# Expert results of a routed block: rows scattered to DRAM, or returned to token order by 0/1 products and added on chip

## The chip, the cores and the metric

One Trainium2 chip, one core. The metric is the device time of the whole program in microseconds (us). Times are the median of several executions; profiles are of one execution, on the same core.

## The reference

One transformer block with 512 tokens of width 1024, float32. The first half (a stick-breaking attention beside an RWKV-7 time mix, gates, an output product, a residual sum) gives `x1`. The change is in the second half, a mixture of experts:

```python
h = rmsnorm(x1, g2) * (1 + sc2) + sh2
# 4 groups of 8 experts: the group of the largest logit, in it the two best experts
combine = sum over the 2 choices of one_hot(expert) * (group_w * top_p)
y = 0
for e in range(32):
    hid = silu(h @ w_up1[e]) * (h @ w_up3[e])       # 1024 -> 512
    y = y + combine[:, e] * (hid @ w_down[e])       # 512 -> 1024
out = x1 + gt2 * rmsnorm(y, g3)
```

The weights of one expert are 1024x512, 1024x512 and 512x1024 float32, 6.29 MB; 32 experts, 201 MB in all, are read from DRAM once.

## The kernel before, in words

The program is five instruction streams (SP, Pool, ScalarE, VectorE, TensorE) that wait for each other on semaphores; their order is written out by hand.

**Blocks.** Each token has two choices, so there are 1024 rows to compute, put together in blocks of up to 64 rows (`CAP`) of one expert. Experts 0 to 29 have one block each (`LOOPED`), then come up to 18 overflow blocks (none with these inputs), then experts 30 and 31: 32 blocks. Three sets of buffers (`NSET`) are used in turn: block n uses set n mod 3. ScalarE stores the normalised rows of x1 to DRAM (`h2_rows`, L974). VectorE works out block and place of each choice from ranks, and TensorE sums two lists over the tokens (L2021): `idx_i`, the token of each place, and `dst_i`, the row of `choice_rows` to which the result goes.

**Loads.** SP loads each block's weights (`load_expert`, L439 to L456) in four parts of 1 MB (L444) and one of 2 MB (L448) or two of 1 MB (L452). The next load into a set is issued when TensorE has used the part: the first half of the up weights (`up_half`), the second (`up_done`), the down weights (`down_done`). All go through SP's one queue (q1).

**A block.** Pool gathers its rows by an indirect DMA (L627). TensorE turns them (`turn_rows`, L2031), VectorE scales them into `hgT` (L1470). TensorE makes the up products (L2042, 16 products of 128x512, each two entries in the trace), ScalarE takes silu (L988), VectorE multiplies (L1475), TensorE turns the product (L2049), VectorE copies it (L1477), and TensorE makes the down products (L2057). The two halves of the 1024 columns stand on partitions 0 to 63 and 64 to 127. ScalarE copies them to `yo` (L995), and Pool scatters `yo` to `choice_rows` in DRAM (L632), with a copy of the index ahead (L653, L663). The buffer of `yo` is used again when its last scatter has landed. TensorE's order is: up of block n, turning of n+1, transposes and down of n. Each set has PSUM banks of its own for up and down.

**The end.** The last block (31) is not scattered. SP waits for all scatters (L558) and reads `choice_rows` back, 4.2 MB (L562). ScalarE weighs the first choice (L1012), VectorE adds the weighed second (L1496), TensorE adds up that sum and the last block's rows in PSUM (L2085, L2091), ScalarE takes the squares' sum and its inverse root (L1016 to L1018), VectorE scales the row out of PSUM (L1501), and Pool (tiles 0 to 2, L673) or VectorE (tile 3, L1511) adds x1. Four stores (L565) end the program. x1 stays in SBUF throughout.

## Time and profile before

| | |
|---|---|
| three executions | 1134.23, 1134.31, 1136.68 us; median 1134.31 |
| the profiled execution | 1133.66 us |
| its span, first to last instruction | 1131.9 us |
| TensorE busy | 992.9 us (88%) |
| VectorE, ScalarE, Pool busy | 428.2, 287.3, 178.7 us |
| read from DRAM, written | 276.62 MB, 12.60 MB |
| queue q1 (SP) | 265.94 MB |
| queue q0 (Pool's indirect DMAs) | 8.40 MB, 5120 packets |

Window times count from the span's start. The expert loop begins at about 628 us; what stands ahead of it is not touched by the change but for buffers. A row of the chain view tells what the end of the program hung on at that moment: an engine's instruction (PE is TensorE), a DMA, or an issue on a queue (SPq is SP's). In group rows the columns are busy us and mean ns of one, then the idle us of the engine ahead of them with what ended it. In timeline rows the columns are start, length, engine, line, instruction, operands, count. DMA rates are in GB/s over all 16 DMA engines of the core; at more than 100% in a queue's share the packets' times overlap.

### The profile page before, as it was taken

The numbers are of one execution on the slowest core, as the hardware profiler recorded it, in microseconds if no ns is written. First come the engines' busy times: TensorE is split into PE (matmuls) and PEld (weight loads), VectorE is DVE, ScalarE is ACT, GpSimd is POOL, SyncE is SP. The second block draws the span as 40 slices with busy tenths as digits, with TensorE's granted clock in tenths as the row PEclk, the third lists the DMA queues.
The fourth block names the chain that finished last, engine by engine and source line by source line (L and its number), as shares of the span: only waits on it lengthen the run. The fifth ranks groups of instructions, "written<-read, shape, count | busy, mean of one in ns | idle before, by whom it ended". The sixth has DMA issues, their size and how long they took to land.

```text
span 1131.9 us, 17069 instructions
## 1 busy us (share of the span) xinstructions
PE 992.9 (88%) x7067; PEld 552.4 (49%) x7067; DVE 428.2 (38%) x853; ACT 287.3 (25%) x447; POOL 178.7 (16%) x239
## 2 busy tenths in 40 slices
PE   3999999999998999999997899977777788777876
PEld 2588478755556676546884433323322232222222
DVE  2477858444467341127437222222211221122124
ACT  3343462366641222245352000000000000000004
POOL 0100000322320100222601112211111111111002
PEclk9899999999999999999998899999999999999999
DMA  9676204205220002334329999999999999999996
GB/s 338 231 248 223 104 3 146 75 24 189 86 75 2 3 5 77 123 124 165 149 112 380 367 398 401 400 399 401 402 410 412 407 406 398 406 399 397 411 415 242
DMA packets 70803, 281.67 MB, mean 249 GB/s; under 512 B 9347, under 2 KB 18861, under 8 KB 46171
## 3 DMA queue, kind: packets, MB, share of 16 engines
q1 hardware_dynamic: 63408, 265.94, 60.6%
q0 software_dynamic: 5120, 8.40, 2.3%
q10 hardware_dynamic: 2218, 6.52, 1.6%
q8 instruction: 43, 0.70, 0.3%
q14 instruction: 14, 0.11, 0.0%
HBM read 276.62 MB, written 12.60 MB: 256 GB/s over the span
## 4 chain that ended last, share of the span: by engine, by line
PE 42%; SPq 30%; DVE 11%; DMA 8%; ACT 4%; issue 3%; POOL 1%; ACTq 0%; DVEq 0%; POOLq 0%
SPq L444 21%; PE ps L1718 7%; SPq L448 6%; PE ps L2042 4%; SPq L452 3%; PE ps L1729 3%; DMA ring<-in_w_up 2%; PE ps L2057 2%; PE ps L1587 2%; PE ps L1588 2%; PE ps L1589 2%; DMA arena<-in_w_mod 2%; PE ps L1830 2%; PE ps L1972 1%; DMA ring<-in_w_mod 1%
## 5 line engine op out<-in xcount | busy, mean ns | idle before, releaser
L2042 PE MATMUL ps<-arena 128*64 128x512 f32 x672 | 151.8, 596 | 35.1 <-DMA arena<-in_w_up 35.1
L1475 DVE TENSOR_TENSOR arena<-arena,ps 128x256 f32<-128x256 f32 x32 | 13.5, 421 | 370.6 <-ACT arena L988 370.6
L1718 PE MATMUL ps<-arena,ring 128*128 128x512 f32 x256 | 118.6, 604 | 0.0
L2042 PEld LDWEIGHTS ps<-arena 128*64 128x64 f32 x672 | 48.8, 137 | 136.6 <-issue 104.5
L2042 PE MATMUL ps<-ring,arena 128*64 128x512 f32 x352 | 79.9, 597 | 19.6 <-DMA ring<-in_w_up 19.6
L2057 PE MATMUL ps<-arena 128*64 128x512 f32 x336 | 78.4, 609 | 19.4 <-DMA arena<-in_w_down 14.2
L988 ACT ACTIVATE arena<-ps 128x256 f32<-128x256 f32 x32 | 12.3, 384 | 264.3 <-PE ps L2042 264.3
L1587 PE MATMUL ps<-h_upper,w_upper 128*128 128x512 f32 (+1 forms) x184 | 74.3, 404 | 4.4 <-POOL h_lower_first L573 4.1
L1589 PE MATMUL ps<-h_upper,w_lower 128*128 128x512 f32 (+1 forms) x184 | 72.7, 395 | 0.0
L1718 PEld LDWEIGHTS ps<-arena,ring 128*128 128x128 f32 x256 | 46.1, 190 | 48.8 <-issue 47.2
L1470 DVE TENSOR_SCALAR arena<-ps,par 128x64 f32<-128x64 f32 x256 | 67.2, 335 | 2.6 <-PE ps L2031 2.6
L995 ACT ACTIVATE arena<-ps 128x512 f32<-128x512 f32 x32 | 19.1, 597 | 182.5 <-PE ps L2057 182.5
L2042 PEld LDWEIGHTS ps<-ring,arena 128*64 128x64 f32 x352 | 25.8, 137 | 72.4 <-issue 38.7
L1588 PE MATMUL ps<-h_lower_first,w_upper 128*128 128x512 f32 (+1 forms) x138 | 55.0, 399 | 0.0
L2057 PEld LDWEIGHTS ps<-arena 128*64 128x64 f32 x336 | 25.2, 139 | 58.2 <-issue 38.8
L2057 PE MATMUL ps<-ring,arena 128*64 128x512 f32 x176 | 43.5, 640 | 10.7 <-DMA ring<-in_w_down 8.3
L653 POOL COPY dst_now<-dst_i 128x1 int32 x27 | 4.8, 178 | 297.2 <-ACT arena L995 297.2
L2031 PEld LDWEIGHTS ps<-cst,arena 64*128 64x128 f32 x256 | 30.7, 201 | 30.6 <-issue 30.6
L582 POOL TENSOR_SCALAR_AFFINE_SELECT arena<-arena 128x128 f32<-128x128 f32 x64 | 32.3, 539 | 66.2 <-DVE arena L1201 48.4
L1587 PEld LDWEIGHTS ps<-h_upper,w_upper 128*128 128x128 f32 (+1 forms) x184 | 34.7, 189 | 15.2 <-issue 6.3
L1589 PEld LDWEIGHTS ps<-h_upper,w_lower 128*128 128x128 f32 (+1 forms) x184 | 34.7, 188 | 8.3
L2031 PE MATMUL ps<-cst,arena 64*128 64x64 f32 x256 | 35.1, 278 | 3.9 <-DMA arena<-h_rows,idx_i 3.9
(388 smaller groups left out, 1605.8 us busy)
## 6 DMA issues: line engine op xcount, KB each, us to landing
arena<-in_w_up SPq DMA_DIRECT2D x84, 1024.0 KB, 28.8
ring<-in_w_up SPq DMA_DIRECT2D x44, 1024.0 KB, 29.1
ring<-in_w_down SPq DMA_DIRECT2D x11, 2048.0 KB, 35.0
arena<-in_w_down SPq DMA_DIRECT2D x11, 2048.0 KB, 32.4
arena<-in_w_down SPq DMA_DIRECT2D x20, 1024.0 KB, 28.4
ring<-in_w_mod SPq DMA_DIRECT2D x6, 2048.0 KB, 8.7
arena<-in_w_mod SPq DMA_DIRECT2D x6, 2048.0 KB, 9.4
ring<-in_w_in SPq DMA_DIRECT2D x6, 2048.0 KB, 8.4
```

The lines of the kernel that those rows point to most:

```text
L444: eng.dma_start(eset_up[u][i][:, 2048 * m:2048 * m + 2048], src).then_inc(w_in_sem[u][m], 16)
L448: eng.dma_start(dst, src).then_inc(w_in_sem[u][m], 16)
L452: eng.dma_start(eset_down[u][i], src[:, i, :]).then_inc(w_in_sem[u][m], 16)
L1470: last = TS(hgT[:, k, :], ps[:, 0, CAP * k:CAP * k + CAP], V("A1", k), V("SH1", k), ALU.mult, ALU.add)
L1587: mm(ps[0:m_, b, :], hi, h_hi[:, k, :], start=(k == 0), stop=False)
L1588: used = mm(ps[0:m_, b, :], hi, h_lo[k], start=False, stop=False)
L1589: last = mm(ps[0:m_, b, :], lo, h_hi[:, k, :], start=False, stop=(k == KD - 1))
L1718: last = mm(ps[:, bank, :], w[:, k, P * (n % 2):P * (n % 2) + P], hT[:, k, :], start=(k == 0), stop=(k == KD - 1))
L1729: last = mm(ps[:, 2 + n % 2, :], chunk("OSB", 4)[:, k, P * n:P * n + P], S4(s_q)[:, k, :], start=(k == 0), stop=(k == FT - 1))
L2031: last = tr(ps[:, 0, CAP * k:CAP * k + CAP], hv[:, k, :], ident[0:CAP, 0:CAP])
L2042: last = mm(ps[64 * hf:64 * hf + 64, UP_BANK[u], :].rearrange("p (m n) -> p m n", m=2), hgT[:, k, :], up_pair(u, k)[:, :, 256 * hf:256 * h ...
L2057: last = mm(ps[64 * hf:64 * hf + 64, DOWN_BANK[u], :], hv2[:, k % 2, k // 2, :], wd[:, k % 2, 512 * hf:512 * hf + 512], start=(k == 0), st ...
```

## The change

Results are no longer scattered to DRAM. For each block VectorE builds a 0/1 matrix `back` (slots of the block by 512 tokens) out of the tokens' slot numbers. The block's results, weighed by the router's factors, are multiplied by it on TensorE (one-pass float32r, four tiles of 128 tokens by 1024), and VectorE adds each tile to an accumulator in SBUF, `acc`. `acc` takes the place of x1, which is read back at the end from `h2_rows` and multiplied by its standard deviation. To keep more digits, the results stand as two parts, an upper (ScalarE) and a lower (VectorE), which both halves of the 128 partitions hold for the same 64 slots. The rows are gathered as before.

```diff
@@ SP: the end
-            sp.wait_ge(none_stored, 16)
-            for u in range(NSET):
-                sp.wait_ge(yo_stored[u], again * 16 + (32 if u == 0 else 16))
+            sp.wait_ge(up_done, NSET * again + NSET)
             for t in range(NT):
-                for ch in range(2):
-                    row = 2 * (T * ch + P * t)
-                    sp.dma_start(fin[t][:, ch, :], ye_dram[row:row + 2 * P, :].rearrange("(p h) n -> p (h n)", h=2)).then_inc(ring_in[t], 16)
+                sp.dma_start(x1_rows[t], h2_dram[P * t:P * t + P, :]).then_inc(h2_moved, 16)
@@ Pool
-            nc.gpsimd.indirect_dma_start(
-                out=ye_dram, out_offset=bass.IndirectOffsetOnAxis(ap=dst_i[:, MAXB - 1:MAXB], axis=0), in_=none, in_offset=None,
-                bounds_check=4 * T - 1, oob_is_err=False).then_inc(none_stored, 16)
+            pool.wait_ge(x1T_done, NT + 1)
+            nc.gpsimd.memset(S(3), 0.0)
+            nc.gpsimd.memset(S(4), 0.0).then_inc(zeroed, 1)
...
                     pool.wait_ge(yo_ready, NSET * it + (u + 1))
-                    nc.gpsimd.tensor_copy(dst_now[:, u:u + 1], dst_i[:, bass.ds(NSET * it + u, 1)]).then_inc(dst_link, 1)
-                    pool.wait_ge(dst_link, NSET * it + (u + 1))
-                    pool.sem_inc(register_pass, 1)
-                    scatter_rows(u, dst_now[:, u:u + 1])
+                    nc.gpsimd.tensor_copy(w_now[:, u:u + 1], w_slot[:, bass.ds(NSET * it + (NSET + u), 1)]).then_inc(w_now_ready, 1)
...
             for t in range(NT - 1):
                 pool.wait_ge(fin_row, t + 1)
-                nc.gpsimd.tensor_tensor(fin[t][:, 1, :], fin[t][:, 1, :], x1[:, t, :], ALU.add).then_inc(first_ready, 1)
+                pool.wait_ge(x1_back, t + 1)
+                nc.gpsimd.tensor_tensor(acc[:, t, :], acc[:, t, :], x1_rows[t], ALU.add).then_inc(first_ready, 1)
@@ ScalarE
-                A(yo[:, u, :], ps[:, DOWN_BANK[u], :], ACT.Copy).then_inc(yo_ready, 1)
+                for a, h in ((0, 0), (HD, 512)):
+                    last = A(yo[a:a + HD, h:h + 512], ps[a:a + HD, DOWN_BANK, :], ACT.Copy, scale=weight[a:a + HD, :])
+                last.then_inc(yo_upper, 1)
...
+            expert_act(NSET * again + (NSET + 1), w_slot[:, LAST:LAST + 1])
+            act.wait_ge(h2_moved, 2 * 16 * NT)
+            for t in range(2):
+                A(x1_rows[t], x1_rows[t], ACT.Copy, scale=std2[:, t:t + 1]).then_inc(x1_back, 1)
+            expert_act(NSET * again + (NSET + 2), w_slot[:, LAST + 1:LAST + 2])
             nc.scalar.preload_act_table_set("natural_log_exp_and_others")
...
             def square_sum(t):
-                link(A(fin_sq[:, t % 2, :].rearrange("p (h n) -> p h n", h=2), whole(t), ACT.Square, accum_out=V("ss", 12 + t)))
+                act.wait_ge(fin_ss, t + 1)
+                link(A(fin_sq, acc[:, t, :], ACT.Square, accum_out=V("ss", 12 + t)))
...
+            for t in range(2, NT):
+                A(x1_rows[t], x1_rows[t], ACT.Copy, scale=std2[:, t:t + 1]).then_inc(x1_back, 1)
@@ VectorE: ahead of the loop
-            TS(dst_i[:, :], where, 2.0, K("half"), ALU.mult, ALU.add).then_inc(dst_ready, 1)
+            link(STT(key, blk_, float(CAP), rr, ALU.mult, ALU.add))
+            for c in range(2):
+                TT(key_diag[:, c], ident3.broadcast_to((P, NT, P)), o1(key[:, NT * c:NT * c + NT]).broadcast_to((P, NT, P)),
+                   ALU.mult).then_inc(factor_ready, 1)
...
+            for i in range(N2):
+                TS(ohw[:, i, :], K("iota64")[:, 0:MAXB], blk_[:, i:i + 1], routf[:, i:i + 1], ALU.is_equal, ALU.mult).then_inc(factor_ready, 1)
@@ VectorE: in the loop
+            def add_back(t, sent):
+                dve.wait_ge(back_done, sent)
+                TT(two(acc[:, t, :]), two(acc[:, t, :]), ps[:, BACK_BANK[t]:BACK_BANK[t] + 2, :], ALU.add).then_inc(back_added, 1)
+            def yo_lower(blocks, weight):
+                dve.wait_ge(yo_upper, blocks)
+                for a, h in ((0, 0), (HD, 512)):
+                    o = HD - a
+                    last = STT(yo[o:o + HD, h:h + 512], ps[a:a + HD, DOWN_BANK, :], weight[a:a + HD, :],
+                               yo[a:a + HD, h:h + 512].bitcast(F32), ALU.mult, ALU.subtract)
+                last.then_inc(yo_ready, 1)
+            def back_rows(u, turn):
...
+                TS(b, key_rows[:, 0, :], slot, None, ALU.is_equal).then_inc(back_step, 1)
+                dve.wait_ge(back_step, turn_steps * turn + (2 * u + 2))
+                STT(b, key_rows[:, 1, :], slot, b.bitcast(F32), ALU.is_equal, ALU.add).then_inc(back_step, 1)
...
+            def expert_dve(before, rows, weight, first=False, last=False):
+                if not first:
+                    add_back(0, NT * before - 3)
+                    add_back(1, NT * before - 2)
+                rows()
+                dve.wait_ge(sil_ready, before + 1)
+                TT(hid, sil, ps[:, UP_BANK, 256:512], ALU.mult).then_inc(hid_ready, 1)
+                dve.wait_ge(ht_done, before + 1)
+                CP(hidT, ps[:, 1, 0:256]).then_inc(ht_ready, 1)
+                if not last:
+                    rows_turned_in(before + 2)
+                if not first:
+                    add_back(2, NT * before - 1)
+                    add_back(3, NT * before)
+                yo_lower(before + 1, weight)
@@ VectorE: the end (order: add 0, add 1, row 0, add 2, row 1, add 3, rows 2 and 3, sum of tile 3)
+            def last_added(t):
+                dve.wait_ge(fin_sum, t + 1)
+                TT(two(acc[:, t, :]), two(acc[:, t, :]), ps[:, FIN_BANK[t]:FIN_BANK[t] + 2, :], ALU.add).then_inc(fin_ss, 1)
             def scaled_row(t):
-                return STT(two(fin[t][:, 1, :]), whole(t), V("rs", 12 + t), row2, ALU.mult, ALU.mult)
+                return STT(two(acc[:, t, :]), two(acc[:, t, :]), V("rs", 12 + t), row2, ALU.mult, ALU.mult)
@@ TensorE
+            def send_back(u, t, bank):
+                for h in range(2):
+                    ins = mm(ps[:, bank + h, :], back[:, u, P * t:P * t + P], yo[:, 512 * h:512 * h + 512], start=True, stop=True)
+                return ins
             def expert_up: behind the first half of the up products
+                        if before is not None:
+                            pe.wait_ge(yo_ready, before)
+                            pe.wait_ge(back_added, NT * before - 3)
+                            for t in range(2):
+                                send_back((u - 1) % NSET, t, BACK_BANK[t]).then_inc(back_done, 1)
             def expert_down: behind the transposes
+                if before is not None:
+                    pe.wait_ge(back_added, NT * before - 1)
+                    for t in (2, 3):
+                        send_back((u - 1) % NSET, t, BACK_BANK[t]).then_inc(back_done, 1)
@@ the end
+            for t in range(NT):
+                send_back(1, t, FIN_BANK[t]).then_inc(fin_sum, 1)
```

The up products of all blocks now use one PSUM bank (2), the down products one (3). TensorE sums the slots' weights (16 products) ahead of turning the first rows, and spreads the tokens' slot numbers over the partitions (two products of 128x512) behind it.

## Rows read from the trace of the kernel before

**Rows 1.** page, busy share of the DMA engines in 40 slices

```profile
DMA  9676204205220002334329999999999999999996
```

**Rows 2.** the chain that ended last, in order of time: start us, us, what

```profile
641.33 6.87 PE ps L2042 x32
...
653.83 6.87 PE ps L2042 x32
...
703.95 2.00 SPq L452
```

**Rows 3.** timeline of SP's queue: start us, us, what, issues

```profile
766.68 6.92 SPq L448 DMA_DIRECT2D ring<-in_w_down  x1
...
910.70 6.56 SPq L448 DMA_DIRECT2D ring<-in_w_down  x1
```

**Rows 4.** timeline of Pool, its indirect transfers (L627 gather, L632 scatter)

```profile
1044.25 0.94 POOL L627 DMA_INDIRECT arena<-h_rows,idx_i  x1 [7.57 <-PE ps L2031]
...
1066.91 1.00 POOL L632 DMA_INDIRECT choice_rows<-arena,dst_now  x1 [0.88 <-POOL dst_now L663]
```

**Rows 5.** DMA view, 1020 to 1060 us, rate in 40 slices of 1 us

```profile
GB/s 418 418 434 426 381 258 270 389 393 418 410 451 426 410 401 418 467 401 442 397 410 291 287 410 410 410 467 410 373 254 320 451 426 418 401 418 434 418 434 410
```

**Rows 6.** DMA view, 1059:1066, then 1066:1074, queue 1: packets, MB, share

```profile
q1 hardware_dynamic: 408, 2.97, 101.7%
...
q1 hardware_dynamic: 443, 3.23, 96.7%
```

**Rows 7.** timeline, before and at the start of the expert loop

```profile
614.96 1.81 DVE L1431 TENSOR_SCALAR arena<-cst,rt 128x50 f32<-128x50 f32 x8
...
628.59 7.03 PE L2042 MATMUL ps<-ring,arena 128*64 128x512 f32 x31
```

**Rows 8.** groups by line and shape

```profile
L900 ACT ACTIVATE ring<-ps,par 128x512 f32<-128x512 f32 x8 | 5.5, 688 | 3.2 <-PE ps L1718 3.1
...
L1012 ACT ACTIVATE arena<-arena,routf 128x1024 f32<-128x1024 f32 x4 | 4.6, 1145 | 3.9 <-DMA arena<-choice_rows 3.9
...
L1294 DVE SCALAR_TENSOR_TENSOR arena<-ps,arena 128x512 f32<-128x512 f32 x4 | 2.8, 692 | 7.8 <-PE ps L1919 7.8
```

**Rows 9.** groups of Pool's instructions by line

```profile
L618 POOL MEMSET arena<- 128x2048 f32 x1 | 1.8, 1821 | 0.0
```

**Rows 10.** window 560:566, TensorE in the output products

```profile
560.00:566.00 6.00, 6.00 (x28) 1.00 0.00 0
```

**Rows 11.** timeline of expert 0

```profile
635.66 0.38 ACT L988 ACTIVATE arena<-ps 128x256 f32<-128x256 f32 x1 [6.27 <-PE ps L2042]
636.08 0.42 DVE L1475 TENSOR_TENSOR arena<-arena,ps 128x256 f32<-128x256 f32 x1 [7.95 <-ACT arena L988]
...
637.46 2.10 DVE L1470 TENSOR_SCALAR arena<-ps,par 128x64 f32<-128x64 f32 x8
...
637.68 3.65 PE L2057 MATMUL ps<-ring,arena 128*64 128x512 f32 x16 [0.59 <-DVE arena L1477]
```

**Rows 12.** timeline of the tail

```profile
1102.40 3.65 PE L2042 MATMUL ps<-arena 128*64 128x512 f32 x16 [1.90 <-DMA arena<-in_w_up]
...
1124.57 1.02 ACT L1016 ACTIVATE arena<-ps 128x1024 f32<-128x1024 f32 x1 [1.30 <-PE ps L2091]
...
1126.27 1.28 DVE L1501 SCALAR_TENSOR_TENSOR arena<-ps,par,raw 128x1024 f32<-128x1024 f32 x1 [1.69 <-ACT par L1018]
1127.59 1.23 DVE L1511 TENSOR_TENSOR arena<-arena 128x1024 f32<-128x1024 f32 x1
```

**Rows 13.** DMA view, 1100 to 1105 us, rate in 40 slices

```profile
GB/s 524 360 492 262 393 524 328 459 262 393 492 360 459 164 295 590 328 361 295 393 361 590 197 262 459 328 328 393 262 328 328 328 328 131 328 328 197 197 131 197
```

**Rows 14.** timeline, Pool and VectorE side by side in the mixer's end

```profile
528.44 1.29 POOL L611 TENSOR_TENSOR wo_lower<-arena,wo_upper 128x512 fp32r<-128x512 f32 x1 [1.81 <-ACT wo_upper L935]
...
528.90 1.38 DVE L1315 TENSOR_TENSOR ring<-ring,arena 128x512 f32<-128x512 f32 x1
```

**Rows 15.** one line of Pool, ns min/median/max

```profile
L673 POOL TENSOR_TENSOR arena<-arena x3: 2342/2346/3321, 1119.3 to 1124.8; 128x1024 f32<-128x1024 f32 x3
```

More of the change, by code:

```diff
@@ L136, in build @@
         wr = sb("wr", [P, KD, NG + E])
+        with (nc.sbuf_tensor("results", [P, D], F32R) as yo, nc.sbuf_tensor("key_rows", [P, 2, T], F32) as key_rows,
+              nc.sbuf_tensor("key_diagonals", [P, 2, NT, P], F32) as key_diag):
+            pass
         h_lo_first = sb("h_lower_first", [P, 6, T], F32R)
@@ L162, in build @@
             pass
+        with nc.sbuf_tensor("under_back", [P, 12 * 2048 + 512], F32), nc.sbuf_tensor("back", [P, NSET, T], F32R) as back:
+            pass
         arena = sb("arena", [P, 17, 2048])
@@ L1436, in _ @@
             link(TS(second, where, float(T), -float(T), ALU.is_ge, ALU.mult))
-            TT(idx_i[:, :], where[0:CAP], second[0:CAP], ALU.add).then_inc(idx_ready, 1)
+            TT(idx_i[:, :], where[0:CAP], second[0:CAP], ALU.add).then_inc(table_ready, 1)
             ov = ovb
@@ new lines, in _ @@
+            rows_turned_in(1)
+            dve.wait_ge(table_done, 3)
+            CP(key_rows[:, :, :], ps[:, BACK_BANK[1]:BACK_BANK[1] + 2, :]).then_inc(back_added, 1)
+            dve.wait_ge(table_done, 2)
+            CP(w_slot, ps[:, BACK_BANK[0], 0:MAXB]).then_inc(table_ready, 1)
+            dve.wait_ge(table_ready, 2)
+            dve.wait_ge(back_added, 1)
+            dve.wait_ge(zeroed, 2)
+            for u in range(NSET):
+                expert_dve(u, lambda: back_rows(u, 0), w_now[:, u:u + 1], first=(u == 0))
@@ new lines, in _, with back_rows_last @@
+            with dve.Fori(0, again) as it:
+                for u in range(NSET):
+                    expert_dve(NSET * it + (NSET + u), lambda: back_rows(u, it + 1), w_now[:, u:u + 1])
+            def back_rows_last(u):
+                b, slot = back[:, u, :], K("slot")[:, NSET + u:NSET + u + 1]
+                link(TS(b, key_rows[:, 0, :], slot, None, ALU.is_equal))
+                STT(b, key_rows[:, 1, :], slot, b.bitcast(F32), ALU.is_equal, ALU.add)
+            for u in range(E - LOOPED):
+                expert_dve(NSET * again + (NSET + u), lambda: back_rows_last(u), w_slot[:, LAST + u:LAST + u + 1],
+                           last=(u == E - LOOPED - 1))
@@ L2056, in expert_down @@
                     for hf in range(2):
-                        last = mm(ps[64 * hf:64 * hf + 64, DOWN_BANK[u], :], hv2[:, k % 2, k // 2, :],
+                        last = mm(ps[64 * hf:64 * hf + 64, DOWN_BANK, :], hv2[:, k % 2, k // 2, :],
                                   wd[:, k % 2, 512 * hf:512 * hf + 512], start=(k == 0), stop=(k == 3))
                 last.then_inc(down_done, 1)
+            for c in range(2):
+                ohr = rview(1168 + 256 * c, 256, 4)
+                for t in range(NT):
+                    pe.wait_ge(factor_ready, 2 * NT + 2 + NT * c + t + 1)
+                    for hf in range(2):
+                        last = mm(ps[64 * hf:64 * hf + 64, BACK_BANK[0], 0:MAXB], ohr[:, t, :], selw[:, c, t, :], start=(c == 0 and t == 0),
+                                  stop=(c == 1 and t == NT - 1))
@@ L2061, in _ @@
+            last.then_inc(table_done, 1)
             turn_rows(0, 1)
+            for c in range(2):
+                pe.wait_ge(factor_ready, 2 * NT + c + 1)
+                last = mm(ps[:, BACK_BANK[1] + c, :], K("ones"), key_diag[:, c].rearrange("p t q -> p (t q)"), start=True, stop=True)
+            last.then_inc(table_done, 1)
             pe.wait_ge(route_ready, 1)
-            steps = pe.value_load(nblk_i[0:1, 0:1], min_val=LOOPED // NSET, max_val=(LOOPED + MAXO) // NSET)
-            pe.wait_ge(sel_ready, 2 * NT + 1)
@@ L2065, in _ @@
-            for hf in range(2):
-                for t in range(NT):
-                    last = mm(ps[64 * hf:64 * hf + 64, 7, P * t:P * t + P], selw[:, t, :], ident, start=True, stop=True,
-                              skip_group_check=True)
-            last.then_inc(idx_done, 1)
-            with pe.Fori(0, steps) as it:
-                for u in range(NSET):
-                    expert_up(u, it)
-                    turn_rows((u + 1) % NSET, it + (1 if u + 1 < NSET else 2))
-                    expert_down(u, it)
@@ new lines, in expert @@
+            def expert(u, turn, before, last=False):
+                expert_up(u, turn, before)
+                if not last:
+                    turn_rows((u + 1) % NSET, turn + (1 if u + 1 < NSET else 2))
+                expert_down(u, turn, before)
+            for u in range(NSET):
+                expert(u, 0, u if u else None)
+            with pe.Fori(0, again) as it:
+                for u in range(NSET):
+                    expert(u, it + 1, NSET * it + (NSET + u))
+            expert(0, again + 1, NSET * again + NSET)
@@ L2107 @@
+            expert(1, again + 1, NSET * again + (NSET + 1), last=True)
+            pe.wait_ge(yo_ready, NSET * again + (NSET + 2))
+            pe.wait_ge(back_added, NT * NSET * again + (NT * (NSET + 1) + 1))
+            pe.sem_inc(register_pass, 1)
+            for t in range(NT):
+                send_back(1, t, FIN_BANK[t]).then_inc(fin_sum, 1)
 _INS = ['x', 'c', 'w_mod', 'b_mod', 'norm_gains', 'w_in', 'gate_bias', 'shift_mu', 'w0', 'w_decay_up', 'a0',
```

201 lines of the change are left out of this document (69 added, 132 removed).

## The prediction

> **What bounds the kernel now.** I read the page's slices first [rows 1]: the reader is to see that the DMA line stands at 9 through nearly all of the second half. Then the chain that ended last, in order of time [rows 2]: up to 704 us it runs through TensorE, one expert every 12.5 us (641.33 to 653.83), and from 703.95 on through SP's queue, which issues the loads of the expert weights. So two regimes: first TensorE eats what was loaded ahead, then it waits for weights. Third, SP's issues [rows 3]: the same load comes back after nine experts in 144.0 us, 16.0 us an expert. TensorE needs 12.5, so it has 3.5 us to spare. Fourth, what the DMA engines do with those 16 us [rows 4 to 6]. An expert's weights are 6.29 MB. In 1059 to 1066, with no indirect transfer, queue 1 moved 2.97 MB in 7 us (0.424 MB/us), which would be 14.9 us an expert [rows 6]. The missing 1.1 us are gather and scatter. The gather of 1044.25 had no scatter near it, and 4 to 6 us later the rate drops to 254 and 320 GB/s; the scatter of 1066.91 leaves no dip [rows 4, 5]. The scatter costs little more than its bytes.
>
> **Removed: the scatters.** Beside the scatter queue 1 moved 3.23 MB in 8 us where 3.39 were due [rows 6]: 0.38 us each. By bytes it is 32 rows of 4 KB, 0.13 MB, 0.31 us. I take 0.34. There are 31 ahead of the last weights (one an expert but the last): 31 x 0.34 = 10.5 us by which the last weights land earlier; ends 9.7 and 11.7. The end above, all of the 1.1 us (34), is spoken against by the gather's own dip; no gain at all would need DMA idle time, and the DMA line shows none [rows 1]. The Pool's issue and copies go too; nobody waits for them but the buffer of the same expert. The gather stays and keeps its dip.
>
> **Added before the loop.** VectorE makes eight more small products (the like took 1.81 us [rows 7]), a key and two 128x512 diagonals (0.69 each [rows 8]), and drops five instructions of about 1.7 us: it ends its routing some 2 us later. TensorE must form the weight table before it turns the first rows, so expert 0 starts at about 629.3 for 628.6 [rows 7]. The Pool clears x1's place (two 128x2048, 1.82 us each [rows 9], 3.6 together) where it issued a scatter before; VectorE waits for that only behind the first turned rows, some 6 us after the Pool may begin: hidden, and if it were not, the first experts would pay it out of the 3.5 us spare of each. The first buffers come free 0.7 us later; in the first 20 us the queue is only 1 to 2 us ahead, so DMA idles 0 to 1.5 us. I take 0.3.
>
> **Added in the loop.** Per expert TensorE gets eight one-pass products of 128x512; the output products show 28 in 6.00 us, 0.22 each [rows 10]. Four stand in the middle of the up products (0.9 us, plainly on TensorE's path), four behind the transposes. From the end of the product with silu (636.50) to the first down product (637.68) pass 1.2 us now [rows 11], half of them idle; the four lengthen that by about 0.4. Period: 12.5 + 0.9 + 0.1 + 0.4 = 13.9 us. VectorE gets four adds of 1024 (1.28 each [rows 12]), two compares of 512 and two subtractions (0.69 each [rows 8]), 7.9 us on top of the 0.42 for the product, as much for a copy, and 2.1 for the turned rows [rows 11]: 10.8 us. ScalarE copies twice with a weight (0.69 each [rows 8]) where it copied once. Who waits: the result is ready 1.4 + 1.4 + 0.2 = 3.0 us after the last down product, and TensorE asks for it after half of the up products, 3.4 us: hidden. Behind the first returns VectorE does 2.6 us of adds and 1.4 of compares, then must be free for the product with silu, which comes 4.8 us later (0.7 of returns, 3.6 of up products, 0.5 to the end of silu): hidden by some 0.8. Bounds: 13.4 if all of the second four hide, 16.0 if none of the eight overlap and each takes twice its 0.22. What decides: TensorE falls behind the weights at 15.0 us (637.3 + 31 P against silu of the last expert at 1102.1, below). At 13.9 it stays covered, with DMA as the cover.
>
> **Added in the tail.** I write the times as they would be without the DMA gain. The last weights end at 1105.0, where the rate has died away [rows 13]. x1 (2.1 MB) is issued behind them on the same queue, 5.0 us at queue 1's own rate [rows 6]: 1110.0. ScalarE waits for all four parts **before the last expert's silu**, then scales two of them (1.145 each [rows 8]): 1112.3. Before, that silu came at 1106.1 (1102.40 + 3.65 [rows 12]). So a wait of 6.2 us is new. Then: silu 0.38, product 0.42, 1.2 and 0.4 more to the first down product, down 3.65 [rows 11], two copies 1.4, two subtractions 1.4, first return 0.6: 1121.7. The table load and two scalings of ScalarE end beside that, at 1123.3. VectorE: two adds to 1124.3; square chain of tile 0 1.70 us (1124.57 to 1126.27 [rows 12]), 1125.0; scaled row 0 to 1126.3; add 2 to 1127.6.
>
> Here a port matters. The Pool's subtraction of 528.44 took 1.29 us; VectorE's sum of two SBUF operands that began at 528.90 was done only 0.55 us after the Pool's end, 1.38 us, where 512 elements with an operand in PSUM took 0.69 [rows 8, 14]. The scaled rows now read both operands from SBUF (before: PSUM), so they exclude the Pool's adds (2.34 us [rows 15]). Pool add 0: 1126.3 to 1128.7; row 1 to 1129.9; add 3 to 1131.2; Pool add 1 to 1132.3; row 2 to 1133.4, row 3 to 1134.7; Pool add 2, which waits by then, to 1137.1; VectorE's last add 1138.2; last output 3.1 us (span end less end of that add, 1128.82 [rows 12]): **1141.3**. With no exclusion it is 1137.5, so the port costs 3.8. The Trainium skill, SBUF — State Buffer, section "SBUF: two separate sides", says the same: VectorE and GpSimd share one port pair, the first to start keeps it for its whole instruction, and a VectorE instruction takes it if it has two SBUF inputs. By that rule the sum ends at 1141.3, by a port that is shared out evenly about 2 us sooner; the trace bears the rule out.
>
> **The sum.** 1141.3 + 0.3 - 10.5 = 1131.1 for a span of 1131.9: -0.8 us. The profiled execution took 1133.66, 0.65 less than the median of 1134.31, so I put it as 1134.31 - 0.8 = 1133.5. Gone are the last scatter's landing and the 4.2 MB of choice rows; what is late next is x1, and then the closing chain of VectorE and Pool.
>
> **Rivals.**
> Tail waits cheaper: x1 lands beside the last weights, or the port does not bite. For it: TensorE itself waits for the last weights. Against it: one queue, in order, and the row of the waiting sum [rows 14]. It would give 4 to 7 us: 1127 to 1130. Chance 0.25.
> Scatter dearer than its bytes: part of the dip is its doing where both stand together. Up to 34 us for 10.5; half of the way, -13: 1121. Against it: the gather alone has its dip, the scatter alone none [rows 4, 5]. Chance 0.08.
> Slower, the loop becomes TensorE's and VectorE's: products, subtraction and adds take turns, and the period passes 15.0 us. For it: five more handovers an expert, cover of only 0.4 to 0.8 us at two of them. At 15.5 us silu of the last expert comes at 637.3 + 31 x 15.5 = 1117.8, and 29.0 us later the end: 1146.8, +14.9: 1149. Chance 0.12.
> The DMA time of the scatters does not come back (idle gaps by late buffers eat it): 1141.6, +9.7: 1144. Chance 0.13.
> My forecast 0.42.
>
> **How the numbers follow.** About 0.3%, 3.4 us, is what a measurement here can tell from no change; 0.8 us is within it. Faster 0.25 + 0.08 = 0.33, same 0.42, slower 0.12 + 0.13 = 0.25. The range leaves out most of the dearest scatter and most of the slow loop: 1124 to 1145. The forecast's own range is 1131 to 1137.
>
> **What would show it.** Right: the DMA line full up to the last weights, SP's same load coming back in 15.6 to 15.7 us, up products of TensorE waiting for weights from about expert 15 on, the last weights some 10 us earlier, ScalarE idle 6 us before the last silu, scaled rows of over 2 us beside the Pool. Wrong: chain through TensorE and VectorE to the end (loop bound), DMA below 9 in the expert stage, no wait for x1, or a period under 15.4 us (scatter dearer).

## The result, and the profile after

| | before | changed |
|---|---|---|
| median | 1134.81 us | 1138.90 us |
| lowest to highest, of 7 each | 1134.23 to 1136.68 | 1138.63 to 1140.87 |
| the profiled execution | 1133.66 | 1140.87 |
| its span | 1131.9 | 1139.3 |

The ratio is 1.0038, interval 1.0026 to 1.0049: slower by some 4 us. 1133.5 was forecast, no change; the result lies within the range, but the time moved, and upwards. In the profiled execution the sum said 1131.1 for the span and 1139.3 was measured: 8.2 us are to be found. Part of that is spread between executions: the profiled one of the changed kernel is the longest of its seven, 2.0 us over the median, and the one before lies 1.2 us under its own. A second profile of the changed kernel, taken with the experiments, has a span of 1137.6 us, and the 1.7 us between the two lie ahead of the first gather.

The page of the changed kernel, its engines, its DMA line, queue 0 and the costliest new group:

```profile
PE 1045.1 (92%) x7311; PEld 584.2 (51%) x7311; DVE 666.9 (59%) x1126; ACT 311.3 (27%) x478; POOL 147.6 (13%) x206
...
DMA  9676203215220002433439999999999999999971
...
q0 software_dynamic: 2560, 4.20, 1.4%
...
L1455 DVE TENSOR_TENSOR arena<-arena,ps 128x1024 f32<-128x1024 f32 x124 | 145.4, 1213 | 53.3 <-PE ps L2068 53.3
```

The second half of the DMA line is as full as before [rows 1], but the last two slices are 7 and 1 where they were 9 and 6: the tail is longer and has nothing to move. Half of queue 0's bytes are gone. VectorE is 239 us busier and TensorE 52 us, and neither is the price: the chain that ended last, in order of time, shows why.

```profile
759.04 3.43 PE ps L2084 x16
...
773.21 3.43 PE ps L2084 x16
...
815.78 4.87 SPq L452
...
1078.07 6.29 SPq L562
1084.41 21.42 DMA arena<-h_rows
...
1106.91 1.13 ACT arena L984
```

One expert on TensorE, from up product to up product, is 14.17 us (759.04 to 773.21; 13.9 forecast, 12.5 before [rows 2]). At 815.78 the chain passes to SP's queue, as it did at 703.95 before. So the loop is still the weights' and not VectorE's. At the other end stands what is new: the chain no longer comes out of the last scatter and the reading of `choice_rows`, it comes out of x1 (`h_rows`, SP's L562) through ScalarE's scaling (L984). The timeline of the tail:

```profile
1095.89 3.65 PE L2084 MATMUL ps<-arena 128*64 128x512 f32 x16
...
1105.85 2.19 ACT L984 ACTIVATE arena<-arena,ST 128x1024 f32<-128x1024 f32 x2 [13.81 <-DMA arena<-h_rows]
...
1108.07 0.38 ACT L967 ACTIVATE arena<-ps 128x256 f32<-128x256 f32 x1
...
1108.96 0.70 PE L2091 MATMUL ps<-cst,arena 128*128 128x128 f32 x2 [9.41 <-DVE arena L1487]
...
1111.30 4.76 PE L2103 MATMUL ps<-arena 128*64 128x512 f32 x16
...
1120.02 2.35 DVE L1526 TENSOR_TENSOR arena<-arena,ps 128x1024 f32<-128x1024 f32 x2 [0.98 <-PE ps L2068]
...
1125.35 2.47 DVE L1531 SCALAR_TENSOR_TENSOR arena<-arena,par,raw 128x1024 f32<-128x1024 f32 x1
...
1131.41 3.31 POOL L654 TENSOR_TENSOR arena<-arena 128x1024 f32<-128x1024 f32 x1 [1.16 <-DVE arena L1531]
...
1132.56 3.25 DVE L1542 TENSOR_TENSOR arena<-arena 128x1024 f32<-128x1024 f32 x1
```

The last up products end at 1099.54 (1095.89 + 3.65), 6.5 us earlier than before (1106.05 [rows 12]). Silu, which needs nothing else, comes at 1108.07: 8.5 us behind them, because ScalarE waits for x1 first. TensorE is idle for 9.41 us, and the last down products behind that take 4.76 us for 3.65 before. Then the scaled row of 2.47 us and the last sum of 3.25 us are the instructions that the Pool's adds hold off, as forecast.

The granted clock of the same stretches (columns: window, its length, busy us of the engines, granted clock, DMA share, GB/s):

```profile
1099.00:1108.00 9.00, 0.55 (x4) 0.00 (x0) 0.00 (x0) 2.15 (x2) 0.00 (x0) 0.74 0.52 209
1108.00:1112.00 4.00, 3.04 (x8) 1.80 (x10) 2.29 (x4) 0.42 (x2) 0.00 (x0) 0.50 0.00 0
```

In TensorE's idle time the granted clock falls (0.74 is the mean of that window) to 0.50, the lower level (1.2 GHz), and the turning and the first down products are made there.

The timeline of the start, between the first gather and expert 0:

```profile
619.62 1.12 POOL L624 DMA_INDIRECT arena<-h_rows,idx_i  x1 [58.23 <-DVE idx_i L1409]
...
623.20 1.83 POOL L633 MEMSET arena<- 128x2048 f32 x1
...
623.82 3.94 DVE L1437 TENSOR_SCALAR SAs<-cst,rt,routf 128x50 f32<-128x50 f32 x8
...
626.88 1.95 PE L2112 MATMUL ps<-SAs,arena 128*64 128x50 f32 x32 [5.24 <-DVE SAs L1437]
...
629.83 3.18 PE L2118 MATMUL ps<-key_diagonals,cst 128*128 128x512 f32 x4
```

Expert 0 starts at 632.95, not at 629.3. The eight factor products took 3.94 us where the like took 1.81 before [rows 7], just while the Pool cleared x1's place; TensorE waited 5.24 us for them, and its key products took 3.18 us. The buffers of the first experts come free later, and the DMA view of 626 to 646 us (40 slices of half a us) shows the gap that this leaves:

```profile
DMA  2109259899899899998900098889999999999999
GB/s 90 41 25 213 33 164 377 377 442 442 361 492 459 360 475 410 410 475 344 426 33 0 0 148 197 254 344 393 459 410 426 410 410 492 393 410 475 393 426 393
```

From 636.5 to 637.5 us nothing moves, and little on either side. In 628 to 650 queue 1 carried 7.69 MB, for 8.67 before.

### The profile page after: what moved, and what is told of

It is laid out like the page before. It is cut to its first block, busy times and chain, and to the rows that moved or that the text cites. A ratio compares the mean times of both kernels' runs of the same rounds, so it can differ in the third digit from the quotient of the medians.

```text
span 1139.3 us, 17967 instructions
## 1 busy us (share of the span) xinstructions
PE 1045.1 (92%) x7311; PEld 584.2 (51%) x7311; DVE 666.9 (59%) x1126; ACT 311.3 (27%) x478; POOL 147.6 (13%) x206
## 4 chain that ended last, share of the span: by engine, by line
PE 51%; SPq 23%; DVE 12%; DMA 6%; ACT 4%; issue 3%; POOL 1%; DVEq 0%; ACTq 0%
SPq L448 15%; PE ps L2084 8%; PE ps L1749 7%; SPq L452 5%; PE ps L2103 5%; PE ps L1760 2%; PE ps L2068 2%; SPq L456 2%; DMA arena<-h_rows 2%; PE ps L1618 2%; PE ps L1619 2%; PE ps L1620 2%; DMA arena<-in_w_mod 2%; PE ps L1861 2%; PE ps L2062 1%
## 5 line engine op out<-in xcount | busy, mean ns | idle before, releaser
L1455 DVE TENSOR_TENSOR arena<-arena,ps 128x1024 f32<-128x1024 f32 x124 | 145.4, 1213 | 53.3 <-PE ps L2068 53.3
L2084 PEld LDWEIGHTS ps<-arena 128*64 128x64 f32 x672 | 47.4, 137 | 104.2 <-issue 99.2
L970 ACT ACTIVATE results<-ps,ST 64x512 fp32r<-64x512 f32 x64 | 43.6, 682 | 181.9 <-PE ps L2103 181.5
L2084 PE MATMUL ps<-ring,arena 128*64 128x512 f32 x352 | 79.9, 596 | 4.7 <-DMA ring<-in_w_up 4.7
L2068 PE MATMUL ps<-results,back 128*128 128x512 f32 x256 | 77.5, 425 | 3.2 <-DVE results L1462 3.2
L1462 DVE SCALAR_TENSOR_TENSOR results<-ps,ST,results 64x512 fp32r<-64x512 f32 x64 | 48.0, 750 | 46.5 <-ACT results L970 46.0
L2068 PEld LDWEIGHTS ps<-results,back 128*128 128x128 f32 x256 | 44.4, 193 | 35.2 <-issue 27.6
L645 POOL COPY ST<-ST 128x1 f32 x27 | 4.9, 183 | 336.2 <-DVE results L1462 336.2
L2103 PEld LDWEIGHTS ps<-arena 128*64 128x64 f32 x336 | 23.1, 138 | 45.4 <-issue 36.9
L1618 PEld LDWEIGHTS ps<-h_upper,w_upper 128*128 128x128 f32 (+1 forms) x184 | 34.5, 188 | 15.3 <-issue 6.3
```

The costliest lines, as they stand in the source:

```text
L1455: TT(two(acc[:, t, :]), two(acc[:, t, :]), ps[:, BACK_BANK[t]:BACK_BANK[t] + 2, :], ALU.add).then_inc(back_added, 1)
L1462: last = STT(yo[o:o + HD, h:h + 512], ps[a:a + HD, DOWN_BANK, :], weight[a:a + HD, :], yo[a:a + HD, h:h + 512].bitcast(F32), ALU.mult, ALU ...
L1618: mm(ps[0:m_, b, :], hi, h_hi[:, k, :], start=(k == 0), stop=False)
L2068: ins = mm(ps[:, bank + h, :], back[:, u, P * t:P * t + P], yo[:, 512 * h:512 * h + 512], start=True, stop=True)
L2084: last = mm(ps[64 * hf:64 * hf + 64, UP_BANK, :].rearrange("p (m n) -> p m n", m=2), hgT[:, k, :], up_pair(u, k)[:, :, 256 * hf:256 * hf + ...
L2103: last = mm(ps[64 * hf:64 * hf + 64, DOWN_BANK, :], hv2[:, k % 2, k // 2, :], wd[:, k % 2, 512 * hf:512 * hf + 512], start=(k == 0), stop= ...
```

## The experiments

They ran in three sets, each with its own executions of the kernel before; a ratio is to those. In the expectations, theory A is the account drawn from these two traces, that the named cause costs what is written there; B is that it costs nothing and the time goes elsewhere. The table puts what their traces say side by side, all counted from the first gather's issue, so that the stage ahead, which ends between 616.4 and 621.1 us in these executions, drops out (each number is a difference of two timeline rows, the last one of the span's end and silu). (Expert 0 of the kernel before begins with an entry of its own at 628.27 us, ahead of the 31 of [rows 7].) Each row of times is one profile, and the table shows how far profiles differ where no edit bears on the number: with the start untouched, the last up products end between 479.92 and 482.08 us, and with the tail untouched the stretch from silu to the end takes 30.58 to 31.34.

| kernel | ratio to before (interval) | start of expert 0 | end of last up products | last silu | from silu to the end |
|---|---|---|---|---|---|
| before | 1 | 9.28 | 487.06 | 487.11 | 25.80 |
| changed | 1.0038 (1.0026 to 1.0049) | 13.33 | 479.92 | 488.45 | 31.23 |
| changed, again | 1.0052 (1.0039 to 1.0066) | 13.36 | 479.92 | 488.43 | 31.26 |
| x1 later | 0.9953 (0.9935 to 0.9970) | 13.92 | 480.78 | 480.83 | 29.15 |
| rows in PSUM | 1.0010 (0.9998 to 1.0022) | 13.92 | 482.08 | 490.60 | 28.39 |
| warm tail | 1.0035 (1.0022 to 1.0048) | 13.50 | 480.96 | 489.47 | 29.58 |
| Pool clears later | 1.0042 (1.0027 to 1.0058) | 11.32 | 479.98 | 488.50 | 31.34 |
| warm start | 1.0052 (1.0033 to 1.0070) | 13.00 | 480.69 | 489.20 | 30.85 |
| both start edits | 1.0037 (1.0024 to 1.0050) | 10.31 | 478.14 | 486.64 | 30.58 |
| x1 later, rows in PSUM | 0.9917 (0.9904 to 0.9930) | 13.31 | 481.32 | 481.37 | 26.23 |
| all four | 0.9898 (0.9879 to 0.9918) | 10.42 | 479.17 | 479.22 | 25.71 |
| before, no scatters | 0.9897 (0.9880 to 0.9913) | 9.86 | 478.73 | 478.78 | 25.63 |

**ScalarE's wait for x1, moved behind the last expert's copies.**

```diff
@@ ScalarE
             expert_act(NSET * again + (NSET + 1), w_slot[:, LAST:LAST + 1])
-            act.wait_ge(h2_moved, 2 * 16 * NT)
-            for t in range(2):
-                A(x1_rows[t], x1_rows[t], ACT.Copy, scale=std2[:, t:t + 1]).then_inc(x1_back, 1)
             expert_act(NSET * again + (NSET + 2), w_slot[:, LAST + 1:LAST + 2])
             nc.scalar.preload_act_table_set("natural_log_exp_and_others")
...
+            act.wait_ge(h2_moved, 2 * 16 * NT)
+            x1_scaled(0); x1_scaled(1); square_sum(0); square_sum(1); x1_scaled(2); square_sum(2); square_sum(3); x1_scaled(3)
```

> The changed kernel, with ScalarE's wait for x1 and all four scalings of x1 moved behind the last expert's copies. Theory A (the wait for x1 holds up the last expert): silu of the last expert comes at about 1099.7 instead of 1108.1 us, TensorE no longer idles 9.4 us and its last down products take 3.65 instead of 4.76 us, so the end comes 9 to 11 us earlier: 1128 to 1130 us. Theory B (the end hangs on x1's transfer itself, whoever waits for it): the wait comes back at the sums with x1, the gain is under 4 us: 1135 or more. Theory C (the longer expert loop is the cause of the loss): the last expert's up products are late already, gain under 2 us: 1137 or more.

Median 1129.88 us. The timeline of its tail:

```profile
1093.55 3.65 PE L2090 MATMUL ps<-arena 128*64 128x512 f32 x16
...
1097.25 0.38 ACT L967 ACTIVATE arena<-ps 128x256 f32<-128x256 f32 x1 [7.56 <-PE ps L2090]
...
1099.50 3.65 PE L2109 MATMUL ps<-arena 128*64 128x512 f32 x16
...
1104.60 1.28 ACT L983 ACT_TABLE_LOAD   x1
1105.90 2.19 ACT L994 ACTIVATE arena<-arena,ST 128x1024 f32<-128x1024 f32 x2
```

Silu comes 0.05 us behind the up products. The down products take 3.65 us, since TensorE no longer stands idle ahead of them. And when ScalarE gets to x1, it starts right behind the table load: x1's landing is hidden altogether. By the ratios the wait cost 9.6 us (0.0085 x 1135); the table has 7.6 us of that at silu (488.45 to 480.83) and 2.1 behind it. The changed kernel's second ratio, 1.0052 from another set, would make it 11.2. That one wait is more than twice the whole loss.

**The last rows kept in PSUM.** The last add, the scaled row and, for tile 3, its sum with x1 take one operand from PSUM, as the kernel before did.

```diff
@@ VectorE
-                TT(two(acc[:, t, :]), two(acc[:, t, :]), ps[:, FIN_BANK[t]:FIN_BANK[t] + 2, :], ALU.add).then_inc(fin_ss, 1)
+                TT(whole(t), two(acc[:, t, :]), whole(t), ALU.add).then_inc(fin_ss, 1)
...
-                return STT(two(acc[:, t, :]), two(acc[:, t, :]), V("rs", 12 + t), row2, ALU.mult, ALU.mult)
+                return STT(whole(t) if t == NT - 1 else two(acc[:, t, :]), whole(t), V("rs", 12 + t), row2, ALU.mult, ALU.mult)
```

> The changed kernel, with the last sums kept in PSUM, so that the square and the scaled rows read PSUM and one SBUF operand; same instructions, same counts. Theory A (VectorE and Pool exclude each other where VectorE has two SBUF operands): scaled rows 1 and 3 take 1.28 us again (2.47 for row 1 now), the last sum 1.2 instead of 3.25, the end 3.5 us earlier: 1135.4. Theory B (the rows are long because of something else, or are not on the path): the lengths stay and the end moves by under 1 us: 1138 or more.

Median 1136.84 us. The timeline of its tail:

```profile
1124.69 6.98 POOL L657 TENSOR_TENSOR arena<-arena 128x1024 f32<-128x1024 f32 x3 [84.26 <-DVE arena L1534]
1125.64 1.28 DVE L1534 SCALAR_TENSOR_TENSOR arena<-ps,par,raw 128x1024 f32<-128x1024 f32 x1
...
1131.13 1.22 DVE L1545 TENSOR_TENSOR arena<-ps,arena 128x1024 f32<-128x1024 f32 x1
```

The same scaled row takes 1.28 us beside the Pool for 2.47, the last sum 1.22 for 3.25, and the Pool makes its three adds in one go. 3.2 us by the ratios (0.0028 x 1135), 2.8 by the table: the port was forecast at 3.8. The table's figure is too low, for the last down products of this profile took 5.35 us for 4.76. From the first of the last adds on (1120.34 us, 1120.02 in the changed kernel) the end comes 3.4 us sooner.

**TensorE kept busy while ScalarE waits for x1.**

```diff
@@ TensorE: the last expert
-            expert(1, again + 1, NSET * again + (NSET + 1), last=True)
+            expert_up(1, again + 1, NSET * again + (NSET + 1))
+            for _ in range(9):
+                mm(ps[:, 0, :], K("ones"), cst[:, 0:512], start=True, stop=True, skip_group_check=True)
+            expert_down(1, again + 1, NSET * again + (NSET + 1))
```

> The changed kernel, with nine unused products of 128x512 between the last expert's up products and its transposes, where TensorE idles 9.4 us (wait for x1). Nothing else is moved. Theory A (the granted clock falls in that idle time and lengthens what follows): last down products 3.65 instead of 4.76 us, the returns behind them shorter, the end 1.5 to 2 us earlier: 1137. Theory B (the products are long because of something else): no change, 1139. The difference between this run and the one with x1's wait moved tells how much of that wait's price is the clock.

Median 1139.34 us. Its clock by windows, the columns as above:

```profile
1099.00:1108.00 9.00, 9.00 (x24) 3.48 (x20) 0.47 (x1) 1.49 (x2) 0.00 (x0) 1.00 0.59 240
1108.00:1112.00 4.00, 2.53 (x13) 1.37 (x14) 2.23 (x4) 1.08 (x2) 0.00 (x0) 1.00 0.00 0
```

The clock stays at 1.00 (2.4 GHz) where it was 0.50, and the stretch from silu to the end is 1.65 us shorter in the trace (29.58 for 31.23). The last down products take 3.65 us for 4.76. That is the price of the clock, and it stands in no term of the forecast; against all profiles with an untouched tail (30.58 to 31.34) it is 1.0 to 1.8 us. In the medians it can't be told from nothing (1.0035 for 1.0038): the forecast gain of 1.5 to 2 us is shown in the trace alone.

**The Pool clears x1's place only when VectorE's factors are ready.**

```diff
@@ Pool
             pool.wait_ge(x1T_done, NT + 1)
+            pool.wait_ge(factor_ready, 4 * NT + 2)
             nc.gpsimd.memset(S(3), 0.0)
```

> The changed kernel, with Pool's two memsets of the accumulator held back until VectorE has made the eight weight factors; one wait more, nothing else. Theory A (a memset of Pool shuts VectorE out of the port while it runs): the eight small products take 1.8 us instead of 3.94, the first expert begins about 2 us earlier (631 instead of 633), DMA idles less at 636 to 639, and the end comes 1.5 to 2 us earlier: 1137. Theory B (the gap in the DMA rate comes from the gathers or from the order of loads, not from the late start): the small products get shorter, but the end does not move by over 0.7 us.

```profile
622.66 1.79 DVE L1438 TENSOR_SCALAR SAs<-cst,rt,routf 128x50 f32<-128x50 f32 x8
...
624.58 1.80 POOL L634 MEMSET arena<- 128x2048 f32 x1 [2.52 <-DVE SAs L1438]
...
626.07 3.78 PE L2119 MATMUL ps<-key_diagonals,cst 128*128 128x512 f32 x4
...
629.78 7.91 PE L2085 MATMUL ps<-ring,arena 128*64 128x512 f32 x32
```

In this timeline of its start the eight products take 1.79 us: the memsets beside them were what held them. (That they do it through a port is the expectation's account; the run shows the hold and not the way.) Expert 0 starts 2.0 us earlier. But TensorE still works at the lower clock (keys 3.78, expert 0's up products 7.91 for 7.09), and neither the end of the last up products (479.98) nor the median (1140.21 us) moves. The mechanism is shown, and the gain in time that A expected is missed.

**Four more unused products ahead of the weight table.**

```diff
@@ TensorE
-            idle_products(2)
+            idle_products(6)
```

> The changed kernel, with four more unused products of 128x512 on TensorE ahead of the weight table, where it idles 5.2 us. Theory A (the clock falls in that idle time): the key products take 1.9 us instead of 3.18, they end before the first rows are scaled, the first expert begins 0.8 us earlier, the end 0.5 to 0.8 us earlier: 1138.2. Theory B (they wait for something else): no change, or later if the unused products hold up the table.

Median 1141.71 us: no gain. VectorE's factors still take 3.95 us, and TensorE has run out of its unused products before they come. The key products take 3.54 us (3.18 in the changed kernel), with the granted clock at 0.56 in 630 to 633 us: the edit did not keep the clock up where they stand, so by itself it says nothing of what the clock costs there.

**Both start edits together, and the changed kernel once more.**

> The changed kernel with the two edits ahead of the loop together (Pool's clearing held back, four more unused products ahead of the weight table); each alone moved nothing. Theory A (each alone is covered by the other: late factors or slow key products): the first expert begins 10.5 us after the first gather's issue instead of 13.3, DMA moves about 1 MB more from 628 to 650 us, and the end comes 2 to 2.5 us earlier than the changed kernel of this call. Theory B (what DMA idles at the start it does not lose in the end): start earlier, end within 0.7 us.

> The changed kernel as it is, for comparison on the same chip. 1138.9 us, ratio to the kernel before 1.0038, if nothing depends on the chip.

The timeline of the start and the DMA view of 626 to 646 us, with both edits:

```profile
621.68 1.79 DVE L1438 TENSOR_SCALAR SAs<-cst,rt,routf 128x50 f32<-128x50 f32 x8
...
625.52 1.98 PE L2119 MATMUL ps<-key_diagonals,cst 128*128 128x512 f32 x4
...
627.79 7.09 PE L2085 MATMUL ps<-ring,arena 128*64 128x512 f32 x32 [0.29 <-DVE arena L1447]
```

```profile
DMA  5799999999998999999899999999999999999999
GB/s 115 279 393 442 393 475 393 426 426 442 426 442 377 475 401 369 254 246 295 328 426 426 442 393 426 426 410 442 426 410 377 426 410 442 410 442 393 426 426 442
```

Factors 1.79, keys 1.98, expert 0 at 10.31 us from the gather for 13.36. The gap is gone, only the gather's own dip is left, and queue 1 carried 8.68 MB in 628 to 650 for 8.00 in the changed kernel of the same set. The last up products end 1.8 us earlier (478.14 for 479.92). The ratios are 1.0037 and 1.0052, 1.7 us apart, but their intervals overlap: the 1.8 us is the traces', one of each.

**The two tail edits together.**

> The changed kernel with the two edits of the tail together (x1's wait behind the last copies, last sums in PSUM). Theory A (the two prices add): 9.6 + 3.2 = 12.8 us less than the changed kernel of this call, about 1126. Theory B (one hides the other): under 11 us less.

Median 1125.89 us; against the changed kernel in the same set 15.3 us (0.0135 x 1135), against its first ratio 13.7. The single edits add to 12.8, so they don't overlap. From silu to the end 26.23 us are left, 0.43 more than before the change.

**The kernel before without its scatters.** 31 of 32 scatters are taken out (the one left is the first, of zeros), and with them ScalarE's wait for their landing; SP then waits for the results of expert 30 and reads `h2_rows` twice where it read `choice_rows`. The results of 31 experts are left out of the output.

```diff
@@ Pool
-                nc.gpsimd.indirect_dma_start(
-                    out=ye_dram, out_offset=bass.IndirectOffsetOnAxis(ap=index, axis=0), in_=yo[:, u, :], in_offset=None,
-                    bounds_check=4 * T - 1, oob_is_err=False).then_inc(yo_stored[u], 16)
+                pass
@@ SP
-                    sp.dma_start(fin[t][:, ch, :], ye_dram[row:row + 2 * P, :].rearrange("(p h) n -> p (h n)", h=2)).then_inc(ring_in[t], 16)
+                    sp.dma_start(fin[t][:, ch, :], h2_dram[P * t:P * t + P, :]).then_inc(ring_in[t], 16)
```

> The kernel before without its 32 scatters of results (the first one, of zeros, stays) and without the waits for their landing; in their place at the end SP waits for the result of the last but one expert and reads h2_rows twice, the same 4.2 MB; the results of 31 experts are left out. It prices the scatters by themselves. Theory A (a scatter costs the DMA engines its bytes, 0.34 us each): the last up weights land 9 to 11 us earlier than at 1102.4, and the end 10 to 11 us plus what the last scatter's landing cost (about 7 us, of which the reads take part): 1117 to 1124 us. Theory B (the scatter's DMA time was idle time anyway, or is returned only in part): the last up weights land under 6 us earlier. Theory D (the scatter is also the cause of part of the dips at the gathers): over 13 us earlier.

Median 1123.76 us. One line each of the DMA view of 650 to 1050 us, of the kernel before, of this one and of the changed one (columns: packets, MB, share of 16 engines):

```profile
q1 hardware_dynamic: 20892, 153.98, 96.3%
```

```profile
q1 hardware_dynamic: 21339, 157.36, 98.4%
```

```profile
q1 hardware_dynamic: 21337, 157.40, 98.4%
```

26 scatters lie in that stretch. Without them queue 1 carries 3.38 MB more, or 3.42 in the changed kernel; the scatters' own bytes are 26 x 0.131 = 3.4 MB. So a scatter costs its bytes and no more, 0.31 us at 0.42 MB/us, and the changed kernel gets all of that back in the loop. The profiles of the changed kernel and its variants carry 156.73 to 157.57 MB in this stretch, which makes it 0.25 to 0.33 us. The last up products start at 1092.87 us for 1102.40, 9.5 us earlier, of which 1.2 are the stage ahead: 8.3 by the table. The expectation also counted on the last scatter's landing, and got nothing there: from silu to the end it is 25.63 us for 25.80.

**All four edits.**

> Four edits to the changed kernel together: x1's wait and scalings behind the last expert's copies; the last sums kept in PSUM; Pool's clearing of the accumulator held back until VectorE has made the weight factors; four more unused products of TensorE ahead of the weight table. Theory A (what the scatters gave back was lost in these four places, and the expert loop itself costs nothing): 1138.9 less 10 less 3.5 less 2.3 to 3: 1122 to 1124 us, some 11 us under the kernel before. Theory C (the expert loop of the change costs time itself): no lower than 1130.

Median 1124.18 us, ratio 0.9898 (0.9879 to 0.9918): 11.6 us faster than the kernel before, and the version that beats both. From silu to the end it needs 25.71 us, as little as the kernel before, and silu stands 7.9 us earlier.

## Why the prediction was wrong

It was wrong by its sign; its mechanism held, and four sizes didn't. In the profiled executions, point by point:

- **Removed: the scatters.** Right in kind: their bytes took time of the DMA engines that the weights need, and the changed kernel's loop gets it back. Mis-sized: 0.34 us each was taken between 0.31 and 0.38, and 31 counted. Measured 0.31, the lower end, and the last of the 31 (issued at 1097.48 us) moves its bytes from 1100 us on, beside the very last weights only. From 650 to 1095 us queue 1 gains 3.90 MB on the kernel before, 9.3 us for 10.5. **1.2 us.**
- **Added before the loop.** This step failed by its reasoning. The memsets were called hidden, because nobody waits for them; what they do to VectorE beside them was not asked. The prediction had VectorE and the Pool in each other's way in the tail, but only for instructions with two SBUF operands, and these products have one. Nor is the stage ahead of the loop untouched but for buffers, as the description of the kernel before has it: the memsets, the factor products and the key products stand in it. The memsets held the factor products (3.94 us for 1.79), TensorE stood idle for 5.24 us and went on at the lower clock, expert 0 started at 632.95 for 629.3, and the DMA engines idled. 0.3 us was taken. Counted 31 us on from the first gather, queue 1 has moved 82.10 MB for 83.33 before: 1.23 MB, 2.9 us at 0.42 MB/us, **2.6 us** more. With both start edits it has moved 83.00 MB, for 82.17 in the changed kernel of the same set: 2.0 us of it come back there. Another **0.6 us** is the first gather itself, 619.62 for 618.99, where executions of one kernel differ by more (617.91 in the second profile of the changed kernel).
- **Added in the loop.** Right. 14.17 us a period against 13.9, TensorE covered by the weights from 816 us on, about expert 13 (15 forecast). The groups by line of 650 to 1050 us show the cover shrink as it should, here the largest one, after first and before second: TensorE's idle time ahead of these up products fell from 28.0 to 9.8 us. With the other groups of up and down products, the idle time ended by a weight's DMA is 14.3 us for 67.7.

```profile
L2084 PE MATMUL ps<-arena 128*64 128x512 f32 x576 | 131.0, 596 | 9.8 <-DMA arena<-in_w_up 9.1
```

```profile
L2042 PE MATMUL ps<-arena 128*64 128x512 f32 x544 | 122.8, 596 | 28.0 <-DMA arena<-in_w_up 28.0
```

- **Added in the tail, x1's landing.** The wait was found and put in the right place, and is the largest single cost, 9.6 us with all that hangs on it. It was sized as 5.0 us of bytes behind the last weights. At 1095 us queue 1 still had 3.56 MB to move, 2.10 of them x1: at full rate that ends at 1103.5. ScalarE's go came at 1105.85. The DMA view of 1090 to 1110 us (half-us slices) shows where it goes: the rate falls from 1101.5 on and dies out at 1105.3, with fewer and fewer of the 16 engines busy (first line), and the go comes half a us behind. **2.4 us**, in no term.

```profile
DMA  9999999999999999999999998755420000000000
GB/s 393 393 459 410 426 410 426 459 393 410 426 410 467 393 401 410 393 451 393 393 401 410 393 369 352 287 238 213 172 115 25 0 0 0 0 0 0 0 0 0
```

- **Added in the tail, behind silu.** 29.0 us were forecast (1131.1 less 1102.1), 31.23 measured: **2.2 us**. 1.65 of it is the clock, by the warm tail. All of it lies ahead of the first of the last adds: from silu to there it is 11.95 us (1108.07 to 1120.02) for 9.4 forecast, and from there to the end 19.3 for 19.6. The wait's length had been priced and its effect on TensorE had not. The port was right in kind, 3.8 forecast and 3.2 to 3.4 measured; the Trainium skill, SBUF — State Buffer, section "SBUF: two separate sides", speaks of a pair of ports held for the whole instruction, and the row of 2.47 us beside the Pool's add (1.28 with an operand in PSUM, in the kernel with the rows there) agrees.

These make 1.2 + 2.6 + 0.6 + 2.4 + 2.2 = 9.0 us, 0.8 more than 1139.3 less 1131.1. One thing runs the other way. At 1095 us queue 1 is 2.40 MB ahead of the kernel before, 5.7 us, which is what the forecast's 10.2 less 1.2, 2.6 and 0.6 leaves; but the last up products end 6.5 us earlier. In the kernel before the last up weights come at the queue's end, where the rate falls from 1101 us on (1090 to 1110 us, half-us slices) and the last scatter's bytes still pass; in the changed kernel x1 stands behind those weights. That **0.8 us** is in no term either. Its reason is read from the two traces, and no run tests it; and each of these sizes rests on one profile of either kernel.

```profile
GB/s 426 393 442 426 426 426 393 442 442 410 426 410 410 426 377 442 393 442 426 410 410 426 377 377 344 353 377 311 279 180 238 254 385 352 418 418 385 401 426 385
```

The terms of the start and of the last stretch follow from one habit: a wait, or an instruction beside the path, was priced by its own length and not by what stands idle or is shut out meanwhile.

**The rivals.** Slow loop: no, 14.17 us. Scatter dearer than its bytes: no, 0.31 us. Tail cheaper: no. Scatters' DMA time not coming back: no for the loop, but its mechanism, late buffers, took 2.9 us at the start. Of the signs named beforehand, SP's same load was to come back in 15.6 to 15.7 us. SP's timeline, first of the changed kernel, then of the one before:

```profile
861.46 6.88 SPq L452 DMA_DIRECT2D ring<-in_w_down  x1
...
1053.55 6.24 SPq L452 DMA_DIRECT2D ring<-in_w_down  x1
```

```profile
862.87 6.84 SPq L448 DMA_DIRECT2D ring<-in_w_down  x1
...
1058.79 6.20 SPq L448 DMA_DIRECT2D ring<-in_w_down  x1
```

Twelve experts take 192.1 us for 195.9, 16.0 us each for 16.3. The step is 0.32 us an expert, a scatter's price once more; its absolute figure was a poor sign, since the 16.0 of [rows 3] was of another stretch.

**What stays open.** Whether the start's gain reaches the end. Its first part is clear: 31 us on from the first gather the three profiles with the memsets held back have moved 82.80 to 83.00 MB, and the six with the start untouched 81.57 to 82.17. The memset edit alone is then 0.70 MB, 1.7 us, ahead of the changed kernel's first profile, and gives it up in the next 400 us, with 156.73 MB for 157.38. The ten profiles of this loop lie between 156.73 and 157.41 MB there, 1.6 us apart, so one trace of each can't follow a gain of that size to the end. Why executions of the same loop differ by that much no run shows.

## What to carry to other kernels

When an operand is re-read from DRAM, put the wait for it behind all work of the waiting engine that doesn't need it: in an in-order stream its place costs more (9.6 us here) than the transfer (5.0). Price a wait by what stands idle behind it too, TensorE's clock among it, and a "hidden" Pool instruction by what VectorE does beside it. A small loss can hide a large gain: the change was worth 11.6 us once its waits were placed, and its first form showed 4 us the other way.

## What was not expected of the hardware

- The Pool's memset, which reads nothing, held VectorE's small SBUF products: eight of 128x50 took 3.94 to 3.95 us beside two memsets of 1.83, in every run that had them together, and 1.79 without them.
- TensorE's clock was at 0.50 after 9.4 us of idle time in the tail, and also after some 5 us of idle time at the start: in the windows there it is 0.50 in 626 to 630 us and 0.62 in 630 to 633, and 1.00 in both with the two start edits. The kernel before has a low stretch there too, 0.50 in 620 to 626 and 0.68 in 626 to 630, but is at 1.00 from 630 on.
- The end of the long queue was not sharp: 3.8 us from the first fall of the rate to the last byte, 0.5 more to the engine that waits.
- A gather and a scatter of like size were not alike: the gather's dip (down to some 250 to 300 GB/s, 4 to 7 us behind its issue) stays when the scatters are gone, with them left out of the kernel before and in the changed one, and the scatters cost their bytes alone.
